# Scores of the decay heads: keys' high and low parts stacked in one product of 128 rows

## What is computed

```python
qk = jax.nn.silu(causal_conv(bqk, conv_w, conv_b))
mq, mk = jnp.split(qk, 2, axis=-1)          # 8 heads of 64 for queries and for keys
...
q = q.astype(f32).reshape(bsz, nh, nc, CHUNK, dk) * (dk ** -0.5)
...
scores = jnp.einsum('bhctd,bhcsd->bhcts', q, k) * jnp.exp(d_log - m_t[..., None])
...
num = jnp.einsum('bhcts,bhcse->bhcte', scores, v) + inter_w[..., None] * jnp.einsum('bhctd,bhcde->bhcte', q, c_prev)
```

## Time and profile before

| | |
|---|---|
| median of 3 runs | 3239.73 us (3238.65 to 3241.39) |
| the profiled execution | 3241.02 us |
| its span in the profile | 3239.2 us |
| granted TensorE clock, mean | 0.999 |
| TensorE busy | 3209.8 us (99%), 15796 products |
| weight loads (PEld) | 2689.9 us, beside the products |
| VectorE, ScalarE, GpSimd busy | 1373.7, 831.2, 2067.5 us |

### The profile page before, as it was taken

How to read it: one execution, slowest core, us unless ns; L and a number is a source line. 1 busy time by engine, 2 the same in 40 slices (tenths; PEclk the granted TensorE clock), 3 DMA queues, 4 the chain that set the end, 5 groups by cost and what they waited for, 6 DMA issues and landing times.

```text
span 3239.2 us, 49284 instructions
## 1 busy us (share of the span) xinstructions
PE 3209.8 (99%) x15796; PEld 2689.9 (83%) x15796; DVE 1373.7 (42%) x2205; ACT 831.2 (26%) x1813; POOL 2067.5 (64%) x2052
## 2 busy tenths in 40 slices
PE   7999999999999999999999999999999999999999
PEld 6888888887888888888888888888888888888887
DVE  6767652236676542256554213111366552132121
ACT  5555340025554420022221002011222220021021
POOL 5555656765556567766666776766665567766665
PEclk9999999999999999999999999999999999999999
DMA  3222222232222222332222232222322222222322
GB/s 121 91 87 83 91 84 91 97 104 76 91 85 91 84 85 97 104 98 83 87 87 78 97 104 90 96 95 97 108 85 85 81 77 94 95 98 97 98 97 98
DMA packets 89648, 298.33 MB, mean 92 GB/s; under 512 B 12592, under 2 KB 13488, under 8 KB 89552
## 3 DMA queue, kind: packets, MB, share of 16 engines
q1 hardware_dynamic: 74592, 271.61, 25.1%
q10 hardware_dynamic: 14960, 25.40, 2.6%
HBM read 282.23 MB, written 2.13 MB: 88 GB/s over the span
## 4 chain that ended last, share of the span: by engine, by line
PE 96%; DVE 1%; DMA 1%; POOL 1%; issue 0%; ACT 0%; ACTq 0%; SPq 0%; DVEq 0%; POOLq 0%
PE bank L566 30%; PE bank L568 30%; PE bank L567 30%; PE bank L671 2%; PE bank L728 1%; PE bank L704 1%; PE bank L783 1%; PE bank L717 1%; PE bank L816 1%; PE bank L666 0%; PE bank L680 0%; DMA raw<-in_w_in 0%; POOL w_lo L550 0%; PE bank L683 0%; DMA g_row<-in_gain 0%
## 5 line engine op out<-in xcount | busy, mean ns | idle before, releaser
L550 POOL TENSOR_TENSOR w_lo<-raw,w_hi 128x512 fp32r<-128x512 f32 x1024 | 1383.7, 1351 | 85.5
L547 POOL TENSOR_SCALAR w_hi<-raw 128x512 fp32r<-128x512 f32 x1024 | 701.2, 685 | 1063.2 <-DMA raw<-in_w_in 720.6
L566 PE MATMUL bank<-h_lo,w_hi 128*128 128x512 f32 (+1 forms) x2912 | 1127.6, 387 | 3.8 <-POOL w_lo L550 3.7
L568 PE MATMUL bank<-h_hi,w_hi 128*128 128x512 f32 (+1 forms) x2912 | 1114.7, 383 | 0.0
L567 PE MATMUL bank<-h_hi,w_lo 128*128 128x512 f32 (+1 forms) x2912 | 1113.4, 382 | 0.0
L566 PEld LDWEIGHTS bank<-h_lo,w_hi 128*128 128x128 f32 x2912 | 548.2, 188 | 109.0 <-POOL w_lo L550 4.9
L568 PEld LDWEIGHTS bank<-h_hi,w_hi 128*128 128x128 f32 x2912 | 547.7, 188 | 107.8
L567 PEld LDWEIGHTS bank<-h_hi,w_lo 128*128 128x128 f32 x2912 | 548.5, 188 | 102.3
L1505 DVE TENSOR_TENSOR x<-x,bank 128x512 f32<-128x512 f32 x64 | 44.0, 687 | 392.0 <-PE bank L568 391.7
L566 PE MATMUL bank<-w_lo,up_hi 128*128 128x512 f32 x512 | 199.6, 390 | 0.0
L568 PE MATMUL bank<-w_hi,up_hi 128*128 128x512 f32 x512 | 199.2, 389 | 0.0
(11 more groups left out here) (285 smaller groups left out, 4272.7 us busy)
## 6 DMA issues: line engine op xcount, KB each, us to landing
raw<-in_w_in SPq DMA_DIRECT2D x288, 512.0 KB, 3.3
raw<-in_w_up SPq DMA_DIRECT2D x64, 512.0 KB, 3.3
raw<-in_w_down SPq DMA_DIRECT2D x64, 512.0 KB, 3.3
raw<-in_w_out_a SPq DMA_DIRECT2D x16, 512.0 KB, 3.2
raw<-in_w_out_b SPq DMA_DIRECT2D x16, 512.0 KB, 3.3
raw<-in_w_o SPq DMA_DIRECT2D x16, 512.0 KB, 3.3
raw<-in_p_ret SPq DMA_DIRECT2D x16, 512.0 KB, 3.3
raw<-in_p_sb SPq DMA_DIRECT2D x16, 512.0 KB, 3.2
```

What stands on the lines that cost most here:

```text
L547: nc.gpsimd.tensor_scalar(m.w_hi[:, slot, w], m.raw[:, slot, w], 1.0, 0.0, ALU.mult, ALU.add).then_inc(s["w_step"], 1)
L550: nc.gpsimd.tensor_tensor(m.w_lo[:, slot, w], m.raw[:, slot, w], m.w_hi[:, slot, w].bitcast(F32), ALU.subtract).then_inc(s["split"], 1)
L566: nc.tensor.matmul(dst, hi, rhs_lo, start=first, stop=False, **more)
L568: return nc.tensor.matmul(dst, hi, rhs_hi, start=False, stop=last, **more)
```

## The change

The keys' high and low parts are stacked in one tile of 128 rows: `yk2[a]` holds for head `a` the high part in the head's own 64 rows and the low part in the other 64. `yq2[a]` holds the queries' high part twice, in both halves. One product over 128 rows then gives keys high by queries high plus keys low by queries high. The product of keys high by queries low stays as one over 64 rows. So `m_scores` has 8 products for a head, not 12.

The rounding moves to ScalarE: a new function `m_stacked` makes four copies of 64 x 512 for the queries and two for the keys, and tells VectorE by `y_copied`. VectorE, which told ScalarE by `y_gated` that the gated tiles are there, makes the low parts by four subtractions of 64 x 512. Two semaphores are new (`y_gated`, `y_copied`), and the counts of VectorE's own steps (`DVE_L1`, `DVE_B`) follow. In memory `yq2_0` and `yk2_0` lie on `sgq` and `sgk`, the sigmoids, and `yq2_1` and `yk2_1` behind the tables of cosines.

```diff
             def m_scores(a):
...
-                    mm = product(mst[sb], m.yk_hi[r, keys], m.yk_lo[r, keys], m.yq_hi[r, tok], m.yq_lo[r, tok],
-                                 True, True)
+                    nc.tensor.matmul(mst[sb], m.yk2[a][r, keys], m.yq_lo[r, tok], start=True, stop=False)
+                    mm = nc.tensor.matmul(mst[sb], m.yk2[a][:, keys], m.yq2[a][:, tok], start=False, stop=True)
                 mm.then_inc(s["bs_done"], 1)
...
+            def m_stacked():
+
+                one, two = slice(0, 64), slice(64, P)
+                act.wait_ge(s["y_gated"], at.at("pair", times=2) + 1)
+                for a, r in enumerate((one, two)):
+                    for half in (one, two):
+                        ins = activation(m.yq2[a][half], m.yq[r], ACT.Copy)
+                ins.then_inc(s["y_copied"], 1)
+                act.wait_ge(s["y_gated"], at.at("pair", times=2) + 2)
+                for a, r in enumerate((one, two)):
+                    ins = activation(m.yk2[a][r], m.yk[r], ACT.Copy)
+                ins.then_inc(s["y_copied"], 1)
...
+                m_stacked()
                 log_exp_tables()
                 first_values()
                 m_decays(0)
...
                     copy_out(m.vTb, s["bvT_ready"])
+                    m_stacked()
                     log_exp_tables()
                     m_decays(0)
                     first_values()
...
                     dve.wait_ge(s["bsig_ready"], at.at("pair", times=2) + 1)
-                    own(stt(m.yq[:], m.yq[:], B_DK ** -0.5, m.sgq[:], ALU.mult, ALU.mult))
+                    stt(m.yq[:], m.yq[:], B_DK ** -0.5, m.sgq[:], ALU.mult, ALU.mult).then_inc(s["y_gated"], 1)
                     dve.wait_ge(s["bsig_ready"], at.at("pair", times=2) + 2)
-                    own(tt(m.yk[:], m.yk[:], m.sgk[:], ALU.mult))
-                    split(m.yq_hi[:], m.yq_lo[:], m.yq[:], s["bqk_ready"])
-                    split(m.yk_hi[:], m.yk_lo[:], m.yk[:], s["bqk_ready"])
+                    tt(m.yk[:], m.yk[:], m.sgk[:], ALU.mult).then_inc(s["y_gated"], 1)
+                    one, two = slice(0, 64), slice(64, P)
+                    dve.wait_ge(s["y_copied"], at.at("pair", times=2) + 1)
+                    for a, r in enumerate((one, two)):
+                        ins = tt(m.yq_lo[r], m.yq[r], m.yq2[a][r].bitcast(F32), ALU.subtract)
+                    ins.then_inc(s["bqk_ready"], 1)
+                    dve.wait_ge(s["y_copied"], at.at("pair", times=2) + 2)
+                    for a, (r, other) in enumerate(((one, two), (two, one))):
+                        ins = tt(m.yk2[a][other], m.yk[r], m.yk2[a][r].bitcast(F32), ALU.subtract)
+                    ins.then_inc(s["bqk_ready"], 1)
```

More of the change, by code:

```diff
@@ L184 @@
 ACT_R = 7
-DVE_L1 = 294
+DVE_L1 = 278
 DVE_A = 17
-DVE_B = 28
+DVE_B = 24
 DVE_L2 = 198
@@ L389, in __init__ @@
         self.yq_lo = place.put("yq_lo", [P, S], F32R)
-        self.yk_lo = place.put("yk_lo", [P, S], F32R)
-        self.yq_hi = place.put("yq_hi", [P, S], F32R)
-        self.yk_hi = place.put("yk_hi", [P, S], F32R)
+        place = Region(nc, o_u + 2 * S * 4, o_rest)
+        self.yq2_0 = place.put("yq2_0", [P, S], F32R)
+        self.yk2_0 = place.put("yk2_0", [P, S], F32R)
+        place = Region(nc, at_cos, nc.sbuf_top)
+        self.yk2_1 = place.put("yk2_1", [P, S], F32R)
+        self.yq2_1 = place.put("yq2_1", [P, S], F32R)
+        self.yq2, self.yk2 = [self.yq2_0, self.yq2_1], [self.yk2_0, self.yk2_1]
         place = Region(nc, o_u + 4 * S * 4, o_rest)
@@ L413 @@
 act_step x_done gain_in rms_ready h_hi_ready prm_in rstd_ready max_ready o_rstd_ready f_in row_ln_ready
-rows_m_ready bsig_ready pcol_ready e_ready b_rstd_ready gate_ready og_ready sA_ready sB_ready mask_in
+rows_m_ready y_gated y_copied bsig_ready pcol_ready e_ready b_rstd_ready gate_ready og_ready sA_ready sB_ready mask_in
 pos_in angles_ready sin_ready lam_sum lam_exp rot_q_in rot_k_in sig_ready yq_ready yk_ready zg_ready table_in
```

## The result

The changed kernel takes 3267.84 us (median of 4 runs, 3264.84 to 3269.34), the kernel before on the same chip 3239.91 (3238.65 to 3241.39). The ratio is 1.0085, with a 95% interval from 1.0072 to 1.0097: 27.9 us more, where 21.8 were forecast, and inside the forecast range of 3248 to 3272. The profiled execution took 3267.81 us with a span of 3266.0, so the spans differ by 26.8 us.

A forecast was written before the change was run, and what follows sets the result against it. TensorE, busy for 99% of the span, was taken as the bound. Switches 12.1, waits 3.9 and 2.8, and clock 3 sum to 21.8 us more; on 3241.02 us, with the median 1.3 lower, that gave 3261.5 us, range 3248 to 3272.

The forecast's parts named there:

- rival (c): Scores on TensorE: switches of rows inside one block are free, a head gains 0.615 us; 3231.3 or 3236.6 us; chance 0.08.
- rival (d): Scores on TensorE: the 64-row product is run as one over the whole array; included in rival (c)'s chance of 0.08.
- The term of the switches: Scores on TensorE: changes between 64 and 128 rows, removed products taken off, cost +0.76 us a head, +12.1 us for 16.
- the fixed part of 0.242 us: Each switch of rows on TensorE: 0.295 - 0.053 = 0.242 us beside the columns' streaming, taken for all widths.
- The lower bound of the same step: Scores on TensorE: if each switch only adds the 0.20 us seen, +9.4 us.
- the estimate: Scores on TensorE: with the skill's 398 cycles or 0.166 us as a switch's fixed part, about +3.6 us; not adopted.
- The waits for the bank: TensorE before the transposes in each hybrid layer's first pair: waits of 3.9 and 2.8 us for bank `misc`.
- Rival (a): Switches cost as read, but first pairs hardly wait, VectorE and GpSimd sharing better: 3249 to 3254 us; chance 0.17.
- VectorE would go first there: Second hybrid layer's first pair: copies end just before GpSimd starts, VectorE goes first, TensorE waits 2.8 us.
- The clock: TensorE behind the two first-pair waits: a lower granted clock costs +3 us, bounds nothing to 8.4 us.
- 2 us for the longer wait and 1 for the shorter: Split of the +3 us for TensorE's lower clock behind the 3.9 and 2.8 us waits, chosen nearer the lower end.
- The other six pairs: Pairs after each layer's first: TensorE's cover of 1 us holds, cost nothing; if gone, perhaps 0.5 us each, 3 together.

The follow-up runs named there:

- The grouped products: Changed kernel with the bank released before the low parts, and each head's four 64-row products put ahead of its four 128-row ones: 3247.3 us, ratio 1.0022.
- The run on the kernel before: Kernel before, with only VectorE's release of the shared bank moved behind the diagonals in a layer's first pair: 3253.79 us, ratio 1.0041.
- the kernel with the waits removed: Changed kernel with zero-filled halves (all score products 128 rows), bank release, queries' copies and second value transposes moved, 32 increments of padding: 3233.53 us, ratio 0.9977.
- the padded kernel before: Kernel before, with 224 semaphore increments added at the start of TensorE's program: 3261.53 us in one run.
- the bank freed earlier: Changed kernel with VectorE's release of the shared bank put ahead of the low parts in a layer's first pair: 3264.93 us, ratio 1.0078.

## Why the forecast was near, point by point

**The direction and the mechanism held.** Fewer products, and slower: what a head gains by four products it loses by changing between 64 and 128 rows. The grouped products show it with the same eight products of a head: 0.19 us for a change inside one block. So rival (c), that only the border between kinds of work costs, is out, and rival (d) too, since the trace names both sizes.

**The term of the switches was too large**, 12.1 us where the timeline shows 8.3. The step that failed is the fixed part of 0.242 us, read from the one border at a head's end and taken for every change: 512 columns at 2.4 GHz are 0.213 us, so it was 0.43 - 0.21 = 0.22 behind 512 and 0.25 - 0.05 = 0.20 behind 128, at the very width where the border had shown 0.242. The seven steps of a head take 320.00 - 317.54 = 2.46 us and not 2.71, and 16 times 0.25 is the whole miss of this term. Why the border at a head's end was dearer than a change inside a block stays open. The lower bound of the same step, +9.4, was nearer. By the Trainium skill ("TensorE: Matmul & The Clock Gate", Single matmul latency) the estimate had been +3.6 us; the trace, with 8.3, lies between the two.

**The waits for the bank came nearly as worked out**, 7.4 us for 6.7. In the first layer the transposes stood at 303.15, forecast was 304.2; nearly all of the difference is that this kernel stood 1 us ahead there (its last product in front of them is at 299.07, before at 300.05), and the turns that VectorE and GpSimd take are in the rows. Rival (a), that they hardly wait, had the switches nearly right and the waits wrong. In the second layer I had 2.8 and read 3.70. The step that failed is that VectorE would go first there: its first subtraction and GpSimd's `w_hi` began within 0.05 us (999.34 and 999.29), and the four took 5.5 us, as in the first layer.

**The clock was too cheap**, 3 us for 6.8. The step that failed is "2 us for the longer wait and 1 for the shorter". No row of before showed how long the low level lasts, and I took a value near the lower end of a range from 0 to 8.4. The run on the kernel before prices it alone: 8.5 us behind two waits of 2.7.

**The stall at the loop's jump was not in the forecast at all**: 5.6 us, some 900 us behind the last instruction that the change touches. That the number of instructions in a program moves such stalls about I didn't know, and the timeline of before shows none there, since its jump of 3.6 us lies under queued products.

**The other six pairs**: nothing forecast, nothing seen. In the changed kernel's list of waits no product of line 770 stands; the cover of 1 us held.

So +21.8 against +27.9 is closer than its terms deserve, and that part is luck: one was 3.8 us too large, another 3.8 too small, and the 5.6 that nobody had counted are most of what is left.

## What to carry to other kernels

Before products are merged into taller ones, count how often the number of rows changes in the new order: a change costs 0.2 us here, nearly a whole product of 512 columns, and grouping by size or filling halves with zeros takes it away. Whatever prepares the new operand needs its own cover on each engine, above all where two take turns, and a wait of 3 us in a tuned stream is to be priced well above its length (with the clock behind it 1.6 to 2.7 times, by the table; 13.6 us for 5.4 where nothing else was changed). When a stretch far from the edit gets slower, look at the sequencer behind a loop's jump before looking at data.

## What the runs showed of the hardware

- **A change between 64 and 128 rows** leaves the weight load open on both sides: 0.43 us from start to start behind 512 columns and 0.25 behind 128, where a steady stream had 0.235 and 0.09. The Trainium skill ("TensorEngine Tiling (Array Packing)", Key Properties) has it that changing the tiling mode drains TensorE; the grouped run agrees, with 0.19 us each.
- **A product of 64 rows is no cheaper than one of 128**: in an unbroken row those of 384 columns stand 0.173 us apart over 64 rows and (301.94 - 301.59) / 2 = 0.175 over 128 in the kernel with the waits removed. A head took 2.38 us with twelve of 64 and their two borders, 1.59 us with eight of 128, half of whose operand was zero in four.
- **The low clock** comes behind most waits of 2.5 to 3.7 us, not behind all: after the first wait of the grouped kernel (2.57 us) and after the 3.20 us at the jump in the padded kernel before, the granted clock stays at 1.00. Where it comes, it costs 1.7, 3.4 or 5.1 us behind waits of the same size (5.1 and 1.7 behind 2.69 and 2.70 us, with the bank freed earlier), and two executions of the changed kernel differ (3.4 and 3.4, then 5.0 and 3.4). What decides between these is open.
- **A jump back in a loop** takes 3.3 to 3.9 us on TensorE's sequencer, hidden as long as enough products are queued; a gap more, in which TensorE idles for 2.8 to 4.6 us, follows or doesn't, by where the code lies.
- **Two-operand work of VectorE and GpSimd takes turns**: 1.4 us for VectorE's subtraction of 64 x 512 and 1.6 us for GpSimd's of 128 x 512 beside it, against 0.69 for a VectorE subtraction of 128 x 512 and 1.29 for GpSimd's.
